# Running sums spread over the partitions by DMAs instead of matmuls, and three changes of order, in a two-part float32 network

## The chip, the cores and the metric

One core of a Trainium2 chip. The metric is the device time of one launch in microseconds, the median over several runs.

## The reference

The input is a sequence of 256 rows of 1024, with 16 learned rows ahead of it in the first part. Two attention layers (an indexer chooses up to 64 keys for each query; one key and value head serves eight query heads; a pooled branch and gates are merged in) are followed by a block of feed-forward, mixer, cross-attention and feed-forward parts. All is float32. The piece of the mixer that the change touches:

```python
x = (xh * dt[..., None]); la = dt * a           # 32 heads in 4 groups, 2 chunks of 128 positions
acs = jnp.cumsum(la, axis=-1)                   # the running sums, per head and chunk
seg = acs[..., :, None] - acs[..., None, :]
decay = jnp.exp(jnp.where(causal, seg, -jnp.inf))
y_diag = jnp.einsum('bcgls,bcgkls,bcsgkp->bclgkp', cb, decay, x)
y_off = jnp.einsum('bclgn,bcgkpn,bcgkl->bclgkp', cc, prev, jnp.exp(acs))
```

## The kernel before, in words

Channels lie on partitions, positions on columns. All weights stream once from HBM as 387 slots of 8 tiles of 128x128 (SyncE, L297). Each slot is split into two float32r parts: ScalarE copies the high part (`whi`, L310), GpSimd subtracts for the low part (`wlo`, L318), up to four slots ahead of TensorE. A `block` is one output tile: 8 (or more) weight tiles, each with three matmuls (high by high L358, high by low L359, low by high L360), or in the wide form two (L385, L388). A block takes one of four main PSUM banks, in rotation, and its `by` names the event that frees the bank. The other four banks (`side_`) serve everything else, also in rotation.

Each engine runs its own program, in order, written out by generators. Work beside the blocks (rotations, attention, the mixer's state part) is a list of generators `side`, and `tick(side)` lets each take one step between two blocks. So the place of a step in an engine's queue is set by the number of `yield`s, the same on all engines by hand.

The change touches these places.

- **The start of the first layer** (`layer_tensor`, l = 0): the blocks go keys, values, first index queries, then the rest. `rope_vector` (L711 scaling, L717 to L722 rotation) frees the keys' bank at its last instruction; `values_vector` (L768) frees the values' bank at once and, two yields on, scales the index weights (L773), for which it waits for ScalarE (L780).
- **Attention** (`attend_scalar`): for each pair of heads an exponential (L924) and, two steps later, the copies of the transposed probabilities (L930, L931) that the second product (L895) reads. One step of the program holds the exponentials of one pair and the copies of another.
- **The mixer's running sums.** `steps_vector` computes `acs`, 32 heads by 256 positions (L1607). ScalarE and VectorE split it in two float32r parts (`acr`, L1637, L1612).
- **The mixer's groups** (`ssd_*`, four groups of eight heads). For each pair of heads (`hp`, one per tick) TensorE multiplies a one-hot column with `acr` and so puts the head's sums on all partitions of a side bank (L1773, two matmuls). ScalarE takes four Relu of differences from it (L1916), an exponential in the bank (L1921) and one of the Relus' results (L1922). VectorE multiplies both (L1843, L1848). Group g runs beside the blocks of group g + 1.
- **The blocks beside it** are six `cv` blocks in three pairs and four `z` blocks. For a pair of `cv` blocks VectorE computes a convolution of four taps (L1706 to L1717), ScalarE a tanh (L1728), VectorE the product (L1734), which frees the bank. In `mixer_scalar` the tanh of the pair before stands behind the tick.

Of the kernel before, what the change touches and what calls it, by code (L numbers as in the profile page):

```python
# [13 lines left out]
T = 272  # L14
# [132 lines left out]
class Scalar(Engine):  # L147
    def begin(self, real):
        self.real, self.activation = real, real.activation
        return self  # L150
# [79 lines left out]
def build(tens, sems, known, wts, small, par, con, mem, out):  # L230
# [531 lines left out]
    def values_vector(e, K):  # L762
# [6 lines left out]
        yield  # L769
        yield  # L770
# [146 lines left out]
    def attend_scalar(e, K, t):  # L917
# [3 lines left out]
        for s in range(8):  # L921
            for hh in (2 * s - 2, 2 * s - 1) if 1 <= s < 5 else ():
                e.wait_ge(*v_step.of("max", l, t, s - 1))
                e.activation(K.L[:, hh, 0:nk], K.L[:, hh, 0:nk], ACT.Exp, bias=K.nm[:, hh:hh + 1],  # L924
                             accum_out=K.sm[:, hh:hh + 1]).then_inc(*s_step.done("exp", l, t, hh))
            for hh in (2 * s - 6, 2 * s - 5) if 3 <= s < 7 else ():
# [5 lines left out]
                    *s_out.done("pt", l, t, hh))  # L932
            yield
# [525 lines left out]
    def ffn_scalar(e, K):  # L1459
# [38 lines left out]
    (zacc, xs0, xs1, bc0, bc1, zs0, zs1, xdt, btok, xw, prev, M, E8, cv0, cv1, cv2, mt0, mt1, mt2, tokm, dtde, acol) = arena(  # L1498
        (8, S), (4, S), (4, S), (2, S), (2, S), (4, S), (4, S), (2, 512), (128,), (512,), (512,), (8, 256),
        (8, 128), (S,), (S,), (S,), (S,), (S,), (S,), (5, 32), (32,), (1,))  # L1500
# [4 lines left out]
    acr, idr = tens["acr"][:, 0:S], tens["acr"][:, S:S + 32]  # L1505
# [54 lines left out]

    def steps_tensor(e):
# [10 lines left out]
    def steps_vector(e):  # L1572
# [38 lines left out]
        e.wait_ge(*s_high.of("acr"))  # L1611
        e.tensor_tensor(acr[32:64, :], acs, acr[0:32, :].bitcast(F), ALU.subtract).then_inc(*v_low.done("acr"))  # L1612
# [6 lines left out]
    def steps_scalar(e):  # L1619
# [11 lines left out]
        e.wait_ge(*v_step.of("acs", 1))  # L1631
        e.activation(dq[:, 0:128], acs[:, 0:128], ACT.Exp, scale=-1.0, bias=acs[:, 127:128]).then_inc(*s_step.done("dden"))
# [108 lines left out]
    def ssd_tensor(e, g):  # L1741
# [25 lines left out]
        for hp in range(4):  # L1767
            o = side_.take(e, "seg", g, hp)
            side_.give(("seg", g, hp), (v_step, ("EC", g, hp)))
            e.wait_ge(*v_low.of("acr"))  # L1770
            for i in range(2):
                hd = 8 * g + 2 * hp + i
                m = e.matmul(o[:, S * i:S * i + S], idr[:, hd:hd + 1].broadcast_to([64, 128]), acr, start=True, stop=True)  # L1773
            m.then_inc(*piece.done("seg", g, hp))
            yield
# [39 lines left out]
    def ssd_vector(e, g):  # L1815
# [24 lines left out]
        for hp in range(5):  # L1840
            if hp:
                e.wait_ge(*s_step.of("E", g, hp - 1))
                e.tensor_tensor(E8[:, 2 * hp - 2:2 * hp, :], later(side_.at("seg", g, hp - 1)), ctb, ALU.mult).then_inc(  # L1843
                    *v_step.done("EC", g, hp - 1))
# [49 lines left out]
    def later(o):  # L1894

        return o.rearrange("p (a s) -> p a s", a=2)[:, :, 128:256]

    def ssd_scalar(e, g):
# [11 lines left out]
        for hp in range(4):  # L1910
            o = side_.at("seg", g, hp)
            e.wait_ge(*piece.of("seg", g, hp))
            for i in range(2):
                for c in range(2):
                    hd = 8 * g + 2 * hp + i
# [146 lines left out]
    def mixer_scalar(e):  # L2062
# [466 lines left out]
```

## Time and profile before

| | |
|---|---|
| median of 3 runs | 1271.03 us (1267.33 to 1271.29) |
| the profiled execution | 1270.99 us, span 1269.2 us |
| TensorE matmul, weight load | busy 98%, 90% |
| VectorE, ScalarE, GpSimd | busy 48%, 56%, 77% |
| DMA | 208.58 MB, 164 GB/s |
| mean granted TensorE clock | 0.995 |

A busy TensorE is one with a matmul in flight; how densely they follow is seen only from their starts in the timeline. The busy time of the other engines is summed over stages: in the mixer's groups VectorE and ScalarE are busier than these means.

### The profile page before, as it was taken

The page shows a single profiled execution, that of the slowest core. Times are in us where ns is not written, and L with a number is a line of the kernel's source. Part 1 is how long each engine was busy: PE and PEld are TensorE (multiplying, and loading weights), DVE is VectorE, ACT ScalarE, POOL GpSimd, SP SyncE. Part 2 cuts the span into 40 slices and gives each one's busy share as a digit, 9 for nine tenths or more (in the row PEclk, how much of TensorE's full clock was granted, in tenths as well). Part 3 has the DMA queues.
Part 4 walks back from the last instruction along what each step waited for, and adds up shares of the span by engine and source line. Part 5 has one row for each costly group of instructions (what it writes and reads, how often), then busy time and mean ns, then how long its engine had stood idle before and what let it go on. Part 6 is the DMA issues. An engine that isn't in the chain of part 4 may idle for free.

```text
span 1269.2 us, 22533 instructions
## 1 busy us (share of the span) xinstructions
PE 1241.6 (98%) x8950; PEld 1141.5 (90%) x8950; DVE 609.7 (48%) x1489; ACT 716.0 (56%) x1347; POOL 978.8 (77%) x774
## 2 busy tenths in 40 slices
PE   6999999999999999999999999999999999999997
PEld 5899899998889888889999999999999888888886
DVE  4476754456656444422755666632135234444312
ACT  5455656465556666545554676674447446666532
POOL 4567658767568999989799766769889767899894
PEclk9999999999999999999999999999999999999999
DMA  6334335444345555555465444445556434555552
GB/s 233 124 126 158 131 129 183 152 148 150 117 135 192 188 183 190 190 181 186 150 200 200 150 134 136 151 147 180 179 176 223 157 125 157 184 190 191 173 194 81
DMA packets 57784, 208.58 MB, mean 164 GB/s; under 512 B 6352, under 2 KB 7632, under 8 KB 57552
## 3 DMA queue, kind: packets, MB, share of 16 engines
q1 hardware_dynamic: 57680, 207.15, 49.2%
q8 instruction: 71, 1.16, 0.4%
q14 instruction: 33, 0.27, 0.1%
HBM read 206.07 MB, written 1.05 MB: 163 GB/s over the span
## 4 chain that ended last, share of the span: by engine, by line
PE 91%; DVE 4%; ACT 2%; issue 1%; DMA 1%; SPq 0%; POOL 0%; DVEq 0%
PE bank L385 22%; PE bank L358 17%; PE bank L360 16%; PE bank L359 16%; PE bank L388 11%; PE bank L895 1%; PE bank L699 1%; PE bank L1789 1%; ACT whi L310 1%; PE bank L905 1%; DMA raw<-w_dram 1%; PE bank L2166 1%; PE bank L2138 1%; PE bank L837 1%; PE bank L2188 1%
## 5 line engine op out<-in xcount | busy, mean ns | idle before, releaser
L318 POOL TENSOR_TENSOR wlo<-raw,whi 128x512 fp32r<-128x512 f32 x770 | 978.6, 1300 | 275.1 <-ACT whi L310 273.3
L310 ACT ACTIVATE whi<-raw 128x1024 fp32r<-128x1024 f32 x387 | 404.3, 1053 | 33.5 <-DMA raw<-w_dram 11.8
L358 PE MATMUL bank<-xx,whi 128*128 128x256 f32 (+1 forms) x1296 | 378.9, 292 | 12.0 <-DVE xx L448 9.4
L360 PE MATMUL bank<-xx,wlo 128*128 128x256 f32 (+1 forms) x1296 | 368.8, 285 | 0.0
L359 PE MATMUL bank<-xx,whi 128*128 128x256 f32 (+1 forms) x1296 | 368.6, 284 | 0.0
L358 PEld LDWEIGHTS bank<-xx,whi 128*128 128x128 f32 x1296 | 246.4, 190 | 21.3 <-issue 11.7
L360 PEld LDWEIGHTS bank<-xx,wlo 128*128 128x128 f32 x1296 | 246.8, 190 | 0.0
L359 PEld LDWEIGHTS bank<-xx,whi 128*128 128x128 f32 x1296 | 246.3, 190 | 0.5
L385 PE MATMUL bank<-xx,whi 128*128 128x512 f32 x704 | 178.9, 396 | 0.0
L358 PE MATMUL bank<-yy,whi 128*128 128x256 f32 (+1 forms) x524 | 151.2, 289 | 0.0
L360 PE MATMUL bank<-yy,wlo 128*128 128x256 f32 (+1 forms) x524 | 148.9, 284 | 0.0
L359 PE MATMUL bank<-yy,whi 128*128 128x256 f32 (+1 forms) x524 | 148.7, 284 | 0.0
L385 PEld LDWEIGHTS bank<-xx,whi 128*128 128x128 f32 x704 | 126.2, 188 | 23.8
L385 PE MATMUL bank<-yy,whi 128*128 128x512 f32 x476 | 121.6, 394 | 0.0
L388 PEld LDWEIGHTS bank<-xx,wlo 128*128 128x128 f32 x704 | 95.2, 188 | 8.0
L358 PEld LDWEIGHTS bank<-yy,whi 128*128 128x128 f32 x524 | 99.8, 190 | 2.6 <-issue 2.5
L385 PEld LDWEIGHTS bank<-yy,whi 128*128 128x128 f32 x476 | 85.4, 189 | 16.3 <-DVE yy L2212 0.5
L359 PEld LDWEIGHTS bank<-yy,whi 128*128 128x128 f32 x524 | 99.8, 190 | 0.1
L360 PEld LDWEIGHTS bank<-yy,wlo 128*128 128x128 f32 x524 | 99.8, 190 | 0.0
L388 PE MATMUL bank<-xx,wlo 128*128 128x256 f32 x704 | 97.4, 280 | 0.0
L1433 DVE TENSOR_TENSOR bank<-bank,ar 128x256 f32<-128x256 f32 x88 | 38.0, 432 | 123.2 <-ACT ar L1464 123.0
L1464 ACT ACTIVATE ar<-bank 128x256 f32<-128x256 f32 x88 | 33.8, 384 | 66.8 <-PE bank L388 66.8
(276 smaller groups left out, 1412.8 us busy)
## 6 DMA issues: line engine op xcount, KB each, us to landing
raw<-w_dram SPq DMA_DIRECT2D x387, 512.0 KB, 3.3
h<-x_dram SPq DMA_DIRECT2D x2, 544.0 KB, 6.2
ar<-mem_dram SPq DMA_DIRECT2D x1, 1024.0 KB, 5.6
out_dram<-h SPq DMA_DIRECT2D x4, 256.0 KB, 2.2
cst<-con_dram SPq DMA_DIRECT2D x1, 721.0 KB, 9.6
cst<-con_dram SPq DMA_DIRECT2D x1, 134.0 KB, 3.4
prm<-par_dram SPq DMA_DIRECT2D x1, 131.0 KB, 3.2
```

The source lines that it names most:

```text
L310: e.activation(whi[:, i % NSPL, :], raw[:, i % NRAW, :], ACT.Copy).then_inc(*whi_done.done(i))
L318: return e.tensor_tensor(wlo[:, q, c0:c1], raw[:, i % NRAW, c0:c1], whi[:, q, c0:c1].bitcast(F), ALU.subtract)
L358: e.matmul(o, wh, both[:, 0, :], start=(i == 0), stop=False)
L359: e.matmul(o, wh, both[:, 1, :], start=False, stop=False)
L360: m = e.matmul(o, wl, both[:, 0, :], start=False, stop=(i == len(feed) - 1))
L385: e.matmul(sums, tiles[-1][3], both, start=(i == 0), stop=(i == end))
L388: m = e.matmul(o[:, 0:n], wl, both[:, 0, :], start=False, stop=(i == end), skip_group_check=True)
L699: e.matmul(o, cst[:, C_PERM:C_PERM + 128], x, start=True, stop=True).then_inc(*piece.done("perm", l, kind, b))
L837: e.matmul(o, K.qiT[p0:p0 + 64, hh // 2, c0:c0 + 128], K.kiT[p0:p0 + 64, 0:nk], start=True, stop=True).then_inc(*piece.done("ix", l, t, hh))
L895: m = e.matmul(ob[half:half + 64, 128 * (hh // 2):128 * (hh // 2) + 128], K.V[0:kn, vi, 0:64], K.PT.at(l, t, hh)[0:kn, i, :], start=(i == ...
L1433: e.tensor_tensor(a, a, K.low.at(kind, K.key, j), ALU.add).then_inc(*v_step.done("sum", kind, K.key, j))
L1464: e.activation(b, K.sums(kind, j)[1], ACT.Copy).then_inc(*s_out.done("low", kind, K.key, j))
```

## The change

Running sums: ScalarE writes `acs` to a DRAM buffer once, and for each pair of heads a DMA from ScalarE's queue reads two rows back onto all 128 partitions, into one of three new buffers, three pairs ahead (`load_run`). The matmuls (L1773) and the split of the sums go. The Relus and the exponential read that buffer; the exponential writes to `E8`, and VectorE multiplies `E8` in place.

Tanh first: `mixer_scalar` puts the tanh of the pair before ahead of the tick. Attention: the copies stand ahead of the exponentials in each step. First layer (l = 0): the values' block comes ahead of the keys', and in both layers the scaling of the index weights comes four yields later. The second layer's blocks keep their order.

```diff
@@ values_vector
-        yield
-        yield
+        for _ in range(6):
+            yield
@@ attend_scalar: the loop of the exponentials is moved behind the loop of the copies
@@ layer_tensor
+    def keys_tensor(e, K):
+        l = K.l
+        block(e, ("kk", l, 0), "w_in", l, [(512, 64, 0), (2688, 64, 64)], K.x_all, T, by=[(v_step, ("rope", l, "kk", 0))])
...
-        block(e, ("kk", l, 0), "w_in", l, [(512, 64, 0), (2688, 64, 64)], K.x_all, T, by=[(v_step, ("rope", l, "kk", 0))])
         if l:
+            keys_tensor(e, K)
             norm_sums(e, N)
         block(e, ("v", l), "w_in", l, [(576, 64, 0), (2752, 8, 64)], K.x_all, T)
         if l == 0:
+            keys_tensor(e, K)
             norm_sums(e, N)
@@ mixer
+    def load_run(e, n):
+        if n < 16:
+            if n >= 3:
+                e.wait_ge(*s_step.of("fall", *divmod(n - 3, 4)))
+                e.wait_ge(*s_step.of("E", *divmod(n - 3, 4)))
+            e.dma_start(runs[n % 3], sums[2 * n:2 * n + 2, :].partition_broadcast(128)).then_inc(sems[f"run{n % 3}"], 16)
@@ steps_scalar
         e.wait_ge(*v_step.of("acs", 1))
+        e.dma_start(sums, acs).then_inc(sems["l_a"], 16)
...
-        e.activation(acr[0:32, :], acs, ACT.Copy).then_inc(*s_high.done("acr"))
-        for i in (0, 1):
-            e.activation(idr[32 * i:32 * i + 32, :], ident[0:32, 0:32], ACT.Copy).then_inc(*s_high.done("idr", i))
+        e.wait_ge(sems["l_a"], 16)
+        for n in range(3):
+            load_run(e, n)
@@ ssd_tensor
         for hp in range(4):
-            o = side_.take(e, "seg", g, hp)
...
-                m = e.matmul(o[:, S * i:S * i + S], idr[:, hd:hd + 1].broadcast_to([64, 128]), acr, start=True, stop=True)
             yield
@@ ssd_vector
-                e.tensor_tensor(E8[:, 2 * hp - 2:2 * hp, :], later(side_.at("seg", g, hp - 1)), ctb, ALU.mult).then_inc(
+                m = E8[:, 2 * hp - 2:2 * hp, :]
+                e.tensor_tensor(m, m, ctb, ALU.mult).then_inc(*v_step.done("EC", g, hp - 1))
@@ ssd_scalar
-            e.wait_ge(*piece.of("seg", g, hp))
+            n = 4 * g + hp
+            o = runs[n % 3]
+            e.wait_ge(sems[f"run{n % 3}"], 16 * (n // 3 + 1))
...
-            e.activation(rise, rise, ACT.Exp).then_inc(*s_step.done("E", g, hp))
+            e.activation(E8[:, 2 * hp:2 * hp + 2, :], o[:, :, 128:256], ACT.Exp).then_inc(*s_step.done("E", g, hp))
             e.activation(M[:, 2 * hp:2 * hp + 2, :], M[:, 2 * hp:2 * hp + 2, :], ACT.Exp, scale=-1.0).then_inc(
                 *s_step.done("M", g, hp))
+            load_run(e, n + 3)
@@ mixer_scalar
                     split_for(e, "cv", cb)
-                    tick(side)
                     silu_scalar(e, due)
                     due = ()
+                    tick(side)
```

ScalarE in the first group's head pairs, before (a `whi` row is a split of weights; L1728 is the tanh of a pair of `cv` blocks; `piece` is an event of TensorE, `v_out` one of VectorE, `w0` the landing of a weight slot):

```order
L1916 ACTIVATE ar<-bank,ar 128x128 [waits piece]
L1916 ACTIVATE ar<-bank,ar 128x128 x3
L1921 ACTIVATE bank<-bank 128x2x128 [waits s_step]
L1922 ACTIVATE ar<-ar 128x512
L310 ACTIVATE whi<-raw 128x1024 [waits w0]
L1916 ACTIVATE ar<-bank,ar 128x128 [waits piece]
L1916 ACTIVATE ar<-bank,ar 128x128 x3
L1921 ACTIVATE bank<-bank 128x2x128 [waits s_step]
L1922 ACTIVATE ar<-ar 128x512
L1728 ACTIVATE ar<-bank 128x256 [waits v_out] x2
```

The same place after the change (L1920, L1923, L1925 are the Relus and the two exponentials, L1743 the tanh, `run0` the landing of a load of the sums):

```order
L1920 ACTIVATE ar<-ar 128x128 [waits run0]
L1920 ACTIVATE ar<-ar 128x128 x3
L1923 ACTIVATE ar<-ar 128x256
L1925 ACTIVATE ar<-ar 128x512 [waits s_step]
L1573 DMA ar<-sums_dram 128x512 [waits s_step]
L310 ACTIVATE whi<-raw 128x1024 [waits w0]
L1743 ACTIVATE ar<-bank 128x256 [waits v_out] x2
L1920 ACTIVATE ar<-ar 128x128 [waits run1]
L1920 ACTIVATE ar<-ar 128x128 x3
L1923 ACTIVATE ar<-ar 128x256
```

The tanh pair moved from behind the second head pair to ahead of it, the wait for TensorE became one for a landing, and a DMA issue follows each pair.

VectorE in the first layer's start, before (L711 scales a block, L717 to L722 are a rotation, L773 the scaling of the index weights):

```order
L768 TENSOR_TENSOR ar<-bank,rows 72x272 [waits product]
L711 TENSOR_TENSOR bank<-bank,rows 128x272 [waits product]
L773 TENSOR_SCALAR ar<-ar 128x2x8 [waits s_out]
L711 TENSOR_TENSOR bank<-bank,rows 128x272 [waits product]
L717 TENSOR_TENSOR ar<-bank,cst 128x272 [waits piece]
L719 SCALAR_TENSOR_TENSOR bank<-bank,prm,cst 128x272
L722 TENSOR_TENSOR ar<-ar,bank 128x272 [waits v_step]
```

After:

```order
L768 TENSOR_TENSOR ar<-bank,rows 72x272
L711 TENSOR_TENSOR bank<-bank,rows 128x272 [waits product] x2
L717 TENSOR_TENSOR ar<-bank,cst 128x272 [waits piece]
L719 SCALAR_TENSOR_TENSOR bank<-bank,prm,cst 128x272
L722 TENSOR_TENSOR ar<-ar,bank 128x272 [waits v_step]
```

L773 left its place ahead of the keys' rotation. On TensorE the third index-query block, at the same time, before (`wlo_done` is the low part of the weights, `v_step` here the end of the keys' rotation):

```order
L758 MATMUL bank<-cst,ar 128x72 x2
L699 MATMUL bank<-ar,cst 128x272 [waits s_step]
L358 MATMUL bank<-xx,whi 128x272 [waits wlo_done,v_step]
L359 MATMUL bank<-xx,whi 128x272
L360 MATMUL bank<-xx,wlo 128x272
```

After:

```order
L758 MATMUL bank<-cst,ar 128x72 x2
L699 MATMUL bank<-ar,cst 128x272 [waits s_step]
L358 MATMUL bank<-xx,whi 128x272 [waits wlo_done]
L359 MATMUL bank<-xx,whi 128x272
L360 MATMUL bank<-xx,wlo 128x272
```

The block no longer waits for VectorE.

## Rows read from the trace of the kernel before

**Rows 1.** The page, part 4: the chain that ended last, by engine.

```profile
PE 91%; DVE 4%; ACT 2%; issue 1%; DMA 1%; SPq 0%; POOL 0%; DVEq 0%
```

**Rows 2.** Waits of TensorE: engine, line, releaser; us in total, times, longest.

```profile
PE bank L895 <- ACT ar L931: 1.1, 2, 0.7
```

**Rows 3.** Timeline of TensorE, blocks without side work: start us, us, instruction.

```profile
693.22 0.28 PE L358 MATMUL bank<-xx,whi 128*128 128x256 f32 x1
...
696.06 0.28 PE L358 MATMUL bank<-xx,whi 128*128 128x256 f32 x1
```

**Rows 4.** The same timeline beside the first group's head pairs.

```profile
709.79 0.50 PE L1773 MATMUL bank<-acr 64*128 64x256 f32 x2
710.22 0.39 PE L358 MATMUL bank<-xx,whi 128*128 128x256 f32 x1
...
717.11 0.39 PE L358 MATMUL bank<-xx,whi 128*128 128x256 f32 x1
...
720.55 0.39 PE L358 MATMUL bank<-xx,whi 128*128 128x256 f32 x1
...
723.51 0.38 PE L358 MATMUL bank<-xx,whi 128*128 128x256 f32 x1
```

**Rows 5.** Timeline of ScalarE in the same stretch.

```profile
712.36 1.05 ACT L310 ACTIVATE whi<-raw 128x1024 fp32r<-128x1024 f32 x1
713.79 1.14 ACT L1916 ACTIVATE ar<-bank,ar 128x128 f32<-128x128 f32 x4 [0.38 <-PE bank L1773]
714.97 0.37 ACT L1921 ACTIVATE bank<-bank 128x256 f32<-128x256 f32 x1
...
715.77 0.65 ACT L1728 ACTIVATE ar<-bank 128x256 f32<-128x256 f32 x2
```

**Rows 6.** Single lines: count, ns min/median/max; the last, of 700:850: busy, mean ns.

```profile
L1929 ACT ACTIVATE ar<-ar x8: 406/408/409, 731.4 to 845.2; 128x256 f32<-128x256 f32 x8
...
L1843 DVE TENSOR_TENSOR ar<-bank,ar x16: 411/418/425, 712.0 to 835.8; 128x256 f32<-128x256 f32 x16
...
L1891 DVE TENSOR_TENSOR yy<-ar,yy x16: 408/419/1520, 750.3 to 866.2; 128x256 fp32r<-128x256 f32 x16
...
L1891 DVE TENSOR_TENSOR yy<-ar,yy 128x256 fp32r<-128x256 f32 x12 | 6.4, 574 | 1.7 <-ACT yy L1946 1.7
```

**Rows 7.** Timeline of VectorE in the stretch of rows 4.

```profile
717.77 0.22 DVE L1706 TENSOR_SCALAR ar<-bank,prm 128x3 f32<-128x3 f32 x1
...
720.49 0.87 DVE L1717 SCALAR_TENSOR_TENSOR bank<-bank,prm,ar 128x256 f32<-128x256 f32 x2
...
721.61 0.68 DVE L1848 TENSOR_TENSOR ar<-ar,bank 128x512 f32<-128x512 f32 x1
723.04 0.75 DVE L1734 SCALAR_TENSOR_TENSOR ar<-ar,bank 128x256 f32<-128x256 f32 x2 [0.75 <-ACT ar L1728]
```

**Rows 8.** The line of the weights' DMAs: issue ns; us to landing.

```profile
L297 SPq DMA_DIRECT2D raw<-w_dram x387: 327/328/997, 0.7 to 1241.4; - x194
...
DMA to landing us min/median/max: 3.1/3.3/10.1
```

**Rows 9.** Timeline of TensorE and of VectorE at the first layer's start.

```profile
32.95 0.39 PE L358 MATMUL bank<-xx,whi 128*128 128x272 f32 x1 [2.12 <-DVE ar L722]
...
30.69 0.63 DVE L773 TENSOR_SCALAR ar<-ar 128x16 f32<-128x16 f32 x1 [3.34 <-ACT ar L780]
```

**Rows 10.** Stretches: us, PE, PEld, DVE, ACT, POOL busy (instructions), granted clock, DMA share, GB/s.

```profile
34.00:38.00 4.00, 4.00 (x21) 3.96 (x20) 0.32 (x2) 0.00 (x0) 1.65 (x2) 0.57 0.34 103
...
314.00:318.00 4.00, 4.00 (x23) 4.00 (x22) 0.14 (x1) 0.00 (x0) 2.40 (x2) 0.57 0.23 76
```

**Rows 11.** Timeline of TensorE and of ScalarE in the second layer's attention.

```profile
350.57 0.94 PE L905 MATMUL bank<-cst,ar 128*16 128x128 f32 x6
...
354.19 0.52 ACT L924 ACTIVATE ar<-ar 128x272 f32<-128x272 f32 x1 [0.23 <-DVE ar L947]
...
355.22 0.25 ACT L930 ACTIVATE ar<-bank 16x128 f32<-16x128 f32 x1
```

More of the change, by code:

```diff
@@ L227, in tick, with build @@
             side.remove(g)
-def build(tens, sems, known, wts, small, par, con, mem, out):
+def build(tens, sems, known, wts, small, par, con, mem, out, sums):
     P, V, A, G, Y = Tensor("pe"), Vector("dve"), Scalar("act"), Pool("pool"), Sync("sp")
@@ L932, in attend_scalar @@
                     *s_out.done("pt", l, t, hh))
+            for hh in (2 * s - 2, 2 * s - 1) if 1 <= s < 5 else ():
+                e.wait_ge(*v_step.of("max", l, t, s - 1))
+                e.activation(K.L[:, hh, 0:nk], K.L[:, hh, 0:nk], ACT.Exp, bias=K.nm[:, hh:hh + 1],
+                             accum_out=K.sm[:, hh:hh + 1]).then_inc(*s_step.done("exp", l, t, hh))
             yield
@@ L1504, in build @@
     dtu, dtv, dtw = (M[0:32, i, :] for i in (0, 1, 2))
-    acr, idr = tens["acr"][:, 0:S], tens["acr"][:, S:S + 32]
+    runs = [sg[:, 2 * k:2 * k + 2, :] for k in range(3)]
     cwh, cbh, snh = (prm[:, PARAMS[n]:PARAMS[n] + w] for n, w in (("cw", 96), ("cb", 24), ("sn", 16)))
@@ L1767, in ssd_tensor @@
         for hp in range(4):
-            o = side_.take(e, "seg", g, hp)
[L1769 to L1772, printed above, removed]
-                m = e.matmul(o[:, S * i:S * i + S], idr[:, hd:hd + 1].broadcast_to([64, 128]), acr, start=True, stop=True)
-            m.then_inc(*piece.done("seg", g, hp))
             yield
@@ L1910, in ssd_scalar @@
         for hp in range(4):
[L1911 to L1912 removed]
+            n = 4 * g + hp
+            o = runs[n % 3]
+            e.wait_ge(sems[f"run{n % 3}"], 16 * (n // 3 + 1))
             for i in range(2):
                 for c in range(2):
[L1915 to L1917 removed]
+                    m = e.activation(M[:, 2 * hp + i, 128 * c:128 * c + 128], o[:, i, 128 * c:128 * c + 128],
+                                     ACT.Relu, scale=-1.0, bias=tokm[:, 2 + c, 2 * n + i:2 * n + i + 1])
             m.then_inc(*s_step.done("fall", g, hp))
[L1919 removed]
+            e.activation(E8[:, 2 * hp:2 * hp + 2, :], o[:, :, 128:256], ACT.Exp).then_inc(*s_step.done("E", g, hp))
             e.wait_ge(*s_step.of("fall", g, hp))
[L1921 removed]
             e.activation(M[:, 2 * hp:2 * hp + 2, :], M[:, 2 * hp:2 * hp + 2, :], ACT.Exp, scale=-1.0).then_inc(
                 *s_step.done("M", g, hp))
+            load_run(e, n + 3)
             yield
@@ L2414, with program @@
           "wlo_done"]
-LOADS = ["l_h", "l_h2", "l_c1", "l_c", "l_p", "l_m", "o"] + [f"w{i}" for i in range(NRAW)]
-def program(nc, wts_shape_decl, small, par, con, mem, out):
+LOADS = ["l_h", "l_h2", "l_c1", "l_c", "l_p", "l_m", "l_a", "run0", "run1", "run2", "o"] + [f"w{i}" for i in range(NRAW)]
+def program(nc, wts_shape_decl, small, par, con, mem, out, sums):
     with ExitStack() as ctx:
@@ L2428, in program @@
             "cst": sb("cst", [128, NCONST]), "prm": sb("prm", [128, NPARAM]), "ar": sb("ar", [128, ARENA]),
-            "acr": sb("acr", [64, S + 32], R), "sq": sb("sq", [128, 2, T]), "rows": sb("rows", [128, 2, T]),
+            "sq": sb("sq", [128, 2, T]), "rows": sb("rows", [128, 2, T]),
             "banks": [ctx.enter_context(nc.psum_tensor(f"bank{i}", [128, 512], F)) for i in range(8)],
         }
-        plan, counted, engines = build(tens, sems, None, None, small, par, con, mem, out)
+        plan, counted, engines = build(tens, sems, None, None, small, par, con, mem, out, sums)
         for name in ("tensor", "vector", "scalar", "pool", "sync"):
@@ L2435, in program @@
         nslots = -(-len(plan) // TILES)
-        _, _, engines = build(tens, sems, counted(), wts_shape_decl(nslots), small, par, con, mem, out)
+        _, _, engines = build(tens, sems, counted(), wts_shape_decl(nslots), small, par, con, mem, out, sums)
         block = ctx.enter_context(nc.Block())
@@ L2472 @@
     mem, out = dram("mem_dram", [128, 8, S]), dram("out_dram", [128, 8, S], "ExternalOutput")
-    plan, nslots = program(nc, lambda n: dram("w_dram", [n, 128, SLOT]), small, par, con, mem, out)
+    sums = dram("sums_dram", [32, S], "Internal")
+    plan, nslots = program(nc, lambda n: dram("w_dram", [n, 128, SLOT]), small, par, con, mem, out, sums)
     mats = {
```

18 lines of the change are left out of this document (3 added, 15 removed).

## The prediction

> **What bounds the kernel now.** I read the chain of waits first: 91% of the span is TensorE, spread over the lines of the weight matmuls [rows 1]. So the question for every part of the change is whether it takes columns or a stall out of TensorE's queue, and whether another engine then holds it up at once. Next the waits of TensorE: they are few, and of those that the change can touch one stands in its own row, the attention's second product waiting for copies of ScalarE, 1.1 us in two places [rows 2]. Third the timeline of the mixer, where the change removes instructions.
>
> **The broadcasts by matmul.** Without side work a block of 24 matmuls takes 2.84 us (693.22 to 696.06) [rows 3]. With two broadcast matmuls behind it, it takes 3.44 us (717.11 to 720.55) [rows 4]; that is 0.60 us for one pair, the switch between their kind of operand and the blocks' included. There are 16 pairs. In each of the four groups the first pair stands behind the state matmul, whose own switch stays, so there I count only the pair itself, 709.79 to 710.22, 0.43 us [rows 4]. Gross: 12 x 0.60 + 4 x 0.43 = 8.9 us of TensorE's queue.
>
> **How much of it is kept.** Banks limit it. The four main banks go round, so the block that begins at 723.51 needs the bank of the block that began at 710.22 [rows 4]. VectorE frees that bank with the first of the two L1734 at 723.04, half of 0.75 us, near 723.4 [rows 7]: there is nothing to spare today. Four pairs earlier, TensorE would be there at 723.51 - 0.43 - 3 x 0.60 = 721.3. When is the bank free then? ScalarE: split of weights from 712.36, 1.05 us; then in the new order both tanh at once, 0.65 us, so to about 714.1. Now the second head pair; it took from 713.79 to 715.77, 1.98 us [rows 5]. Its four Relu and its exponential now read SBUF; the nearest pair of rows is 0.37 us for an exponential from PSUM [rows 5] and 0.41 for a square from SBUF [rows 6], so I add 0.04 for each of five and call it 2.2: to 716.3. VectorE multiplies the decays (the second of the two 0.68 us, L1848 [rows 7]), to 717.0, and its convolution of the next pair of blocks takes what it took from 717.77 to 721.36, 3.6 us [rows 7]: to 720.6. Behind it come again the two multiplications, which ended 0.93 us after the convolution (722.29 against 721.36), and the first L1734, 0.4 us [rows 7]; with 0.16 for a port wait (next part) the bank is free at about 722.1 to 722.2. TensorE waits some 0.9, say 1.0 us, for it in each of groups 0 to 2. The last group runs beside the merge gates' blocks, whose banks ScalarE alone frees: no stall. Kept: 8.9 - 3.0 = **5.9 us**. The ends are 8.9 (no stall) and 2.3 (as if those three groups kept today's cadence: 8.9 less 3 x 2.2).
>
> **The multiplication in SBUF (L1843).** It read PSUM and SBUF, 0.42 us and never over 0.43. Now both inputs lie in SBUF, where GpSimd works most of the time. The nearest row is L1891, the same operation and size with two SBUF inputs: median 0.42, longest 1.52 us, and a mean of 0.57 [rows 6]. I take the mean, 0.16 more, and hold 1.1 more for the range. The Trainium skill, in "SBUF — State Buffer", section "SBUF: two separate sides", says that such a VectorE instruction and a GpSimd one exclude each other for a whole instruction. By that rule this change puts 16 exclusions into the tightest chain of the mixer. Row L1891 agrees, with its 1.52 against 0.42; taken at its full length each time, the rule makes the time that of rival 3.
>
> **The transfers.** Three loads of 256 KB follow the write of the sums, and 13 more come one for each head pair, each three head pairs ahead, thus at least 3 x 2.84 = 8.5 us before use. A weight tile of 512 KB lands in 3.3 us, the slowest transfer of that line in 10.1 [rows 8]. I take them as hidden behind those three blocks; if one took 10.1 us, ScalarE would wait 1.6 us for it, up to 21 us for 13. The same 2 KB go to 128 partitions, which no row shows. An issue takes 0.33 us on SyncE [rows 8]; on ScalarE it stands behind the exponential of 512 columns that is still running, so I take 0, the other end being 16 x 0.33 = 5 us on an engine that is off the chain except in the three stalls above (there 3 x 0.33 us each at worst). In exchange two copies and two fills on ScalarE go and one subtraction on VectorE; they bounded nothing, 0 us.
>
> **The first layer's start.** TensorE idles 2.12 us before the block at 32.95 until L722, the end of the keys' rotation [rows 9]: that block, the third of the index queries, takes the bank of the first block, which was the keys'. With the values' block first, that bank is free when the values are scaled, long before. The keys' bank is then wanted one block later, 3 us on, and VectorE reaches the rotation earlier too, as it no longer stands 3.34 us idle before L773 [rows 9], which moves behind. Gain **2.1 us**, with no new waiter. Behind this idle time the granted clock falls to 0.57 over 34 to 38 us [rows 10], between its levels of 2.4 and 1.2 GHz. 4 us at 0.57 are 1.7 us lost. Without the idle time ahead I expect no fall: **1.7 us**, likely but not sure. In the second layer, the keys stay first; 0.
>
> **Copies before exponentials.** The transposes of the first heads ran at 350.57, ScalarE took the exponentials at 354.19 and the copies at 355.22 [rows 11], and TensorE waited for those. Turned round, the copies end about 1.0 us earlier. Both places of [rows 2] have this form: **1.1 us**. The later exponentials are read one block later; 0.
>
> **The sum.** 5.9 + 2.1 + 1.7 + 1.1 = 10.8 us. The profiled execution took 1270.99 us, beside its span of 1269.2, and the median is 1271.03, so one base serves both: 1271.0 - 10.8 = **1260.2 us**.
>
> **Rivals.**
> 1. The clock falls all the same, or at another place: the fall near 314 us [rows 10] stands behind another idle time, that the change does not touch: what lets a fall come is not in my hands. Then 1261.9. Chance 0.15.
> 2. The saved matmuls are only waited out: the three groups keep their cadence, since VectorE and ScalarE hand the banks over with nothing to spare. For it: the 723.4 against 723.51. Against: the tanh no longer stands behind a head pair, and the head pairs no longer wait for TensorE. Time: 1271.0 - (2.3 + 2.1 + 1.7 + 1.1) = 1263.8. Chance 0.12.
> 3. The port: every such multiplication loses 1.1 us. Two lie in each of the three critical chains, so the stall grows by about 2 us a group: 1260.2 + 6 = 1266.2. Against: the mean of L1891 is far from its longest. The rule of the page above would let GpSimd be held up too; no wait for it stands in this stage today. Chance 0.05.
> 4. Slower: the loads land late. ScalarE then stands at its wait in front of the Relu with the next tanh and the next split of weights behind it, so the banks stay taken and TensorE stops. It decides from 8.5 us of landing on; the gain of 10.8 us is used up when 13 loads each cost 0.83 us, thus at 9.3 us, and it is over 0.3% slower at about 9.6. At 10.1 us: 1260.2 + 21 = 1281. For it: a landing of 10.1 exists [rows 8]. Against: the median is 3.3 for twice the bytes. Chance 0.04. "DMA: Bandwidth & Descriptors" of the Trainium skill, section "Latency and other measured facts", gives HBM access as 0.2 us on average and 2 at high load; this would leave the loads hidden, and no row of this kernel shows such a broadcast.
> 5. The forecast itself keeps 0.64.
>
> **How the numbers follow.** 0.3% is 3.8 us, about what a measurement of this kernel can tell from no change. Rivals 1 and 2 and most of the forecast lie below 1267.2. Range: down to 1255.5, where the 3.0 us of stall and the second clock fall (1.7) are gone as well; up to 1266.0, where rivals 1 and 2 come together (1265.5) with a little of the port. Within 0.3% lie rival 3 together with 1 or 2 (1267.9 and more), a mild form of 4, and what I have not thought of: 0.06. Slower is rival 4, 0.04, and faster the rest, 0.90.
>
> **What would show it.** Right: no broadcast matmul, a block pitch near 2.84 us in the head pairs, and one TensorE wait of about 1 us in each of three groups, ended by L1734's successor; no wait at 31 us, and a granted clock of 1.00 there; no wait for the copies at 127 and 356 us. Run loads landing in 2 to 5 us. Wrong: ScalarE idle until a load of the sums; multiplications of 0.42 us that last over 1 us in most cases; a new stall of TensorE outside the cv blocks, or a total above 1267.

## The result, and the profile after

| | before | after |
|---|---|---|
| median of 5 runs, us | 1270.62 (1267.33 to 1271.29) | 1263.48 (1261.66 to 1264.37) |
| ratio to before, 95% interval | | 0.9948 [0.9931, 0.9964] |
| profiled execution: span / time, us | 1269.2 / 1270.99 | 1262.3 / 1264.1 |

The change makes the kernel 0.5% faster; 7.1 us by the medians, 6.9 us by the two spans. The forecast was 10.8 us, to 1260.2. The result lies inside the range of 1255.5 to 1266.0, but 3.3 us above the value itself. Two terms make that distance: stalls of TensorE that are longer than forecast, which can be read and in part undone, and a gain in granted clock that did not come.

The page of the changed kernel, part 4 (the chain that ended last, by engine), against [rows 1]: VectorE's share rose from 4% to 6%.

```profile
PE 90%; DVE 6%; ACT 2%; issue 1%; DMA 1%; SPq 0%; POOL 0%; DVEq 0%
```

Waits of TensorE after the change (engine, line, releaser; us in total, times, longest). The row of [rows 2], L895 waiting for the copies, and the wait for L722 of [rows 9] are gone. A wait of 5.5 us in three places is new.

```profile
PE bank L358 <- DVE ar L1749: 5.5, 3, 2.0
```

Timeline of TensorE in the first group, and the same stall in the next two groups. The blocks beside the head pairs now follow one another in 2.84 us (710.34 to 713.18), the pitch of a bare block in [rows 3], where [rows 4] had 3.44. The next block should then begin at 713.18 + 2.84 = 716.02; it begins at 717.61, **1.59 us late**. The same reckoning gives 2.18 us in groups 1 and 2, thus 5.95 us in all. (The idle time in the rows is a little less, since the previous matmul is counted busy to its end.)

```profile
710.34 0.28 PE L358 MATMUL bank<-xx,whi 128*128 128x256 f32 x1
...
713.18 0.28 PE L358 MATMUL bank<-xx,whi 128*128 128x256 f32 x1
...
717.61 0.38 PE L358 MATMUL bank<-xx,whi 128*128 128x256 f32 x1 [1.43 <-DVE ar L1749]
...
755.14 0.38 PE L358 MATMUL bank<-xx,whi 128*128 128x256 f32 x1 [2.02 <-DVE ar L1749]
...
794.25 0.38 PE L358 MATMUL bank<-xx,whi 128*128 128x256 f32 x1 [2.02 <-DVE ar L1749]
```

Timeline of VectorE ahead of the first of these stalls, the stretch that answers to [rows 7]. The first of the two L1749 (the multiplication with the tanh, L1734 before) frees the bank. Ahead of it stand the convolution, then L1852 and L1856 (L1843 and L1848 before). This L1852 lasts 1.26 us in place of 0.42, and the one ahead of the convolution 0.86.

```profile
710.49 0.86 DVE L1852 TENSOR_TENSOR ar<-ar 128x256 f32<-128x256 f32 x1 [0.99 <-ACT ar L1923]
...
714.59 0.87 DVE L1732 SCALAR_TENSOR_TENSOR bank<-bank,prm,ar 128x256 f32<-128x256 f32 x2
715.37 1.26 DVE L1852 TENSOR_TENSOR ar<-ar 128x256 f32<-128x256 f32 x1
716.55 0.67 DVE L1856 TENSOR_TENSOR ar<-ar,bank 128x512 f32<-128x512 f32 x1
717.15 0.74 DVE L1749 SCALAR_TENSOR_TENSOR ar<-ar,bank 128x256 f32<-128x256 f32 x2
717.81 0.41 DVE L1852 TENSOR_TENSOR ar<-ar 128x256 f32<-128x256 f32 x1
```

The groups of VectorE by line (count; busy us, mean ns; idle before): the mean of L1852 is 698 ns. L1899 is the line that was L1891 in [rows 6].

```profile
L1899 DVE TENSOR_TENSOR yy<-ar,yy 128x256 fp32r<-128x256 f32 x16 | 13.7, 893 | 1.6 <-ACT yy L1950 1.6
L1852 DVE TENSOR_TENSOR ar<-ar 128x256 f32<-128x256 f32 x16 | 11.2, 698 | 5.4 <-ACT ar L1923 5.4
```

What makes an L1852 long shows when GpSimd's low parts of the weights (L318) are laid beside it. First GpSimd, then VectorE, in group 1 of the changed kernel.

```profile
752.60 1.27 POOL L318 TENSOR_TENSOR wlo<-raw,whi 128x512 fp32r<-128x512 f32 x1 [0.45 <-ACT whi L310]
753.84 1.45 POOL L318 TENSOR_TENSOR wlo<-raw,whi 128x512 fp32r<-128x512 f32 x1
```

```profile
752.83 1.32 DVE L1852 TENSOR_TENSOR ar<-ar 128x256 f32<-128x256 f32 x1
```

L1852 begins 0.23 us behind the start of a GpSimd instruction that ends at 753.87, and ends at 754.15, 0.28 us later. This is no accident of one place. I laid all 32 executions of L1852 and L1899 beside GpSimd's. Half of them, 16, begin while an L318 runs and has over 0.15 us left: each of these ends 0.279 to 0.286 us behind the end of that L318. The other 16 take 0.409 to 0.426 us. So the duration of such an instruction is not a spread around a mean; it is set by how much of GpSimd's instruction is left when it begins. Laid out in the same way, the nine traces of this document hold 111 such instructions that begin inside an L318, and 109 of them end 0.277 to 0.287 us behind it. The other two are in `tick_first`, one each in groups 1 and 2: they are recorded as beginning 0.07 us behind the L318, take their 0.41 us, and it is the L318 that takes 1.64 us. So at such a distance the record of the starts does not tell which of the two will be held up; another L1852 of that kernel, 0.07 us behind its L318, took 1.52 us.

```profile
756.63 1.64 POOL L318 TENSOR_TENSOR wlo<-raw,whi 128x512 fp32r<-128x512 f32 x1 [1.60 <-ACT whi L310]
```

```profile
756.71 0.41 DVE L1852 TENSOR_TENSOR ar<-ar 128x256 f32<-128x256 f32 x1
```

The transfers, by the line of their issue (issue ns min/median/max; us to landing): they were as hidden as taken, with no wait for them anywhere.

```profile
L1573 ACTq DMA_DIRECT2D ar<-sums_dram x16: 326/327/454, 644.9 to 820.6; - x16
...
DMA to landing us min/median/max: 3.4/4.0/5.1
```

The granted clock in the profiled execution of the changed kernel (stretches as in [rows 10]) is 1.00 at 34 us and at 310 to 318 us, where the one of before had its two falls, but 0.62 at 26 to 30 us and 0.57 at 756 to 760 us. That makes two falls ahead of the last blocks before and two after, at other places; a share of 1.00 is the level of 2.4 GHz, and within a fall the clock is at 1.2 GHz.

```profile
22.00:26.00 4.00, 2.28 (x15) 1.91 (x14) 2.22 (x9) 1.46 (x3) 2.67 (x4) 0.95 0.74 236
26.00:30.00 4.00, 4.00 (x22) 4.00 (x22) 1.14 (x3) 2.17 (x5) 2.39 (x2) 0.62 0.43 154
...
34.00:38.00 4.00, 4.00 (x33) 3.92 (x32) 2.08 (x6) 1.34 (x2) 2.77 (x3) 1.00 0.23 58
310.00:318.00 8.00, 7.72 (x61) 6.28 (x62) 3.42 (x10) 4.16 (x15) 2.54 (x2) 1.00 0.41 133
752.00:756.00 4.00, 1.98 (x17) 1.77 (x16) 4.00 (x9) 3.96 (x10) 2.84 (x3) 1.00 0.67 236
756.00:760.00 4.00, 4.00 (x25) 3.87 (x25) 3.86 (x11) 1.75 (x4) 3.61 (x3) 0.57 0.67 200
```

### The profile page after: what moved, and what is told of

Read it like the earlier page. It is cut to its first block, busy times and chain, and to the rows that moved or that the text cites. A ratio compares the mean times of both kernels' runs of the same rounds, so it can differ in the third digit from the quotient of the medians.

```text
span 1262.3 us, 22496 instructions
## 1 busy us (share of the span) xinstructions
PE 1232.8 (98%) x8918; PEld 1137.6 (90%) x8918; DVE 613.1 (49%) x1488; ACT 717.0 (57%) x1344; POOL 979.5 (78%) x774
## 4 chain that ended last, share of the span: by engine, by line
PE 90%; DVE 6%; ACT 2%; issue 1%; DMA 1%; SPq 0%; POOL 0%; DVEq 0%
PE bank L385 22%; PE bank L358 16%; PE bank L360 15%; PE bank L359 15%; PE bank L388 11%; PE bank L895 1%; PE bank L699 1%; PE bank L905 1%; ACT whi L310 1%; PE bank L1797 1%; PE bank L912 1%; DVE ar L1727 1%; DMA raw<-w_dram 1%; PE bank L2170 1%; PE bank L2142 1%
## 5 line engine op out<-in xcount | busy, mean ns | idle before, releaser
L318 POOL TENSOR_TENSOR wlo<-raw,whi 128x512 fp32r<-128x512 f32 x770 | 979.3, 1300 | 267.0 <-ACT whi L310 265.1
L358 PE MATMUL bank<-xx,whi 128*128 128x256 f32 (+1 forms) x1296 | 379.2, 293 | 15.4 <-DVE xx L448 9.5
L358 PEld LDWEIGHTS bank<-xx,whi 128*128 128x128 f32 x1296 | 247.0, 191 | 23.4 <-issue 12.6
L358 PE MATMUL bank<-yy,whi 128*128 128x256 f32 (+1 forms) x524 | 151.2, 289 | 0.0
L358 PEld LDWEIGHTS bank<-yy,whi 128*128 128x128 f32 x524 | 99.8, 190 | 2.6 <-issue 2.5
```

What stands on the lines that cost most here:

```text
L318: return e.tensor_tensor(wlo[:, q, c0:c1], raw[:, i % NRAW, c0:c1], whi[:, q, c0:c1].bitcast(F), ALU.subtract)
L358: e.matmul(o, wh, both[:, 0, :], start=(i == 0), stop=False)
```

## The experiments

Seven kernels, in two sets. The first four (`mixer_only` to `e_psum`) ran beside 17 executions of the kernel before with a median of 1269.06 us, the last three beside 23 with 1270.56 us; in the result's own runs it was 1270.62. So a comparison between a kernel of these sets and the changed kernel is safer by the ratios to before than by the medians; where both are given they differ by up to 1.1 us. Every kernel computes the whole reference. Theory A is: the changed kernel's distance from the forecast is the new stall, the stall is set by L1749's place in VectorE's queue, and L1852, with both inputs in SBUF, makes the stall long by waiting for GpSimd.

### The mixer's part alone, and the rest alone

`mixer_only`, from the changed kernel:

```diff
@@ values_vector
-        for _ in range(6):
-            yield
+        yield
+        yield
@@ attend_scalar: the loop of the exponentials goes back ahead of the loop of the copies
@@ layer_tensor
+        keys_tensor(e, K)
...
-            keys_tensor(e, K)
```

> The change with the first layer's start and the attention's order undone; only the mixer's part (sums by DMA, tanh first) is left. Theory A (the traces of before and after add up part by part): three TensorE stalls of 1.6, 2.2 and 2.2 us ahead of the first z block, and the mixer gives 3.9 us of its 8.9, less or more 1.5 for a clock fall. The waits at 31 us (2.1) and for the copies (0.7 and 0.35) are back. Time about 1270.6 - 3.9 = 1266.7, 1.5 less or more by where the clock falls. Rival B (the mixer's part is a loss and the other two edits carry the gain): not below 1270.

Measured: 1267.05 us (11 runs), ratio to before 0.9984 [0.9974, 0.9994], span 1265.0. Waits of TensorE:

```profile
PE bank L358 <- DVE ar L1748: 5.5, 3, 2.0
...
PE bank L358 <- DVE ar L722: 1.7, 1, 1.7
...
PE bank L895 <- ACT ar L931: 1.1, 2, 0.7
```

`start_attn`, from the kernel before, is the complement: the values' block first, L773 later, copies first, and nothing of the mixer.

```diff
@@ values_vector
-        yield
-        yield
+        for _ in range(6):
+            yield
@@ attend_scalar: the loop of the exponentials is moved behind the loop of the copies
@@ layer_tensor
-        block(e, ("kk", l, 0), "w_in", ...)
+        def keys():
+            block(e, ("kk", l, 0), "w_in", ...)
         if l:
+            keys()
...
         if l == 0:
+            keys()
```

> The kernel before with the two other edits alone: values' block ahead of the keys' and L773 later, copies ahead of exponentials. Theory A: the idle time of 2.1 us at 31 us and the two of 0.7 and 0.35 for the copies are gone, 3.4 us with the 0.2 around them, 1267.2. The clock falls once for 3.4 us soon after the idle time at 23 us instead of at 34 us, so that term gives 0, not 1.7; whether the fall at 314 us stays is open (1.5 us). Rival B (removing the idle time removes a fall as well, as I had forecast): granted clock 1.00 from 24 to 40 us and about 1265.5.

Measured: 1265.69 us (5 runs), ratio 0.9968 [0.9956, 0.9981], span 1264.1. Both waits are gone, and the second fall of the clock with them; the first one only moved ahead, to 26 us:

```profile
26.00:30.00 4.00, 4.00 (x22) 4.00 (x21) 1.14 (x3) 2.08 (x5) 2.41 (x3) 0.57 0.39 137
310.00:318.00 8.00, 7.72 (x61) 6.29 (x61) 3.31 (x10) 4.15 (x14) 2.54 (x2) 1.00 0.41 132
```

What follows: the two halves are 0.16% and 0.32%, together 0.48%, against 0.52% for the whole change; they add up. The mixer's half, with 5.9 of the forecast's 10.8 us, is the smaller one on the chip. The three stalls belong to it alone and do not depend on the rest. By the ratio the mixer's half gains 2.0 us (0.8 to 3.3) where 3.9 was expected; the time of 1267.05 came near the expected 1266.7 only because the kernel before was 1.6 us faster in this set. Laid beside before, the profiled execution does gain 4.0 us between 700 and 866 us, and it loses elsewhere: TensorE's clock stays low for 6.8 us from 311.7 us, against 3.4 us before. `start_attn` went as theory A expected, with the fall at 314 us gone besides, which had been left open.

### The tanh behind the side work again

`tick_first` keeps the loads but takes back the order of ScalarE:

```diff
@@ mixer_scalar
                     split_for(e, "cv", cb)
+                    tick(side)
                     silu_scalar(e, due)
                     due = ()
-                    tick(side)
```

> The change with the tanh of the pair before behind the head pair again. Theory A (the tanh's place counts, since the bank is freed by the product behind it): in the first group the tanh of the first pair comes at about 710.5 instead of 708.3 and that of the second about as late as 717.9 instead of 715.1, so the bank of the 12th block is free about 1 to 2 us later: stalls of 2.5 to 4 us in each of three groups, and 3 to 5 us more than the change in all. Rival B (VectorE alone sets the release, since the tanh is done by the time its two multiplications are): stalls as in the change, within 0.5 us.

Measured: 1266.13 us (6 runs), ratio 0.9975 [0.9964, 0.9987]. Six stalls in place of three:

```profile
PE bank L358 <- DVE ar L1749: 7.7, 6, 1.9
```

and in group 1 VectorE waits for the tanh, with a long L1852 in the same round:

```profile
748.23 0.75 DVE L1749 SCALAR_TENSOR_TENSOR ar<-ar,bank 128x256 f32<-128x256 f32 x2 [2.27 <-ACT ar L1743]
748.90 0.76 DVE L1899 TENSOR_TENSOR yy<-ar,yy 128x256 fp32r<-128x256 f32 x2
749.57 1.52 DVE L1852 TENSOR_TENSOR ar<-ar 128x256 f32<-128x256 f32 x1
```

What follows: the due tanh first is worth about 2.7 us by the medians (1266.13 against 1263.48) and 3.4 by the ratios. Theory A's direction is right and its size at the lower end of what it said (3 to 5 us), but groups 1 and 2 each have two stalls, and group 0 stalls for less than the 2.5 us expected. Without the early tanh the removed matmuls bring 0.25% together with all the rest.

### One input of L1852 back in PSUM

`e_psum`: the exponential of the decays is written to the PSUM bank of the state matmul, free by then, and L1852 reads it there. The loads, the matmuls and the order stay those of the changed kernel; ScalarE gets one wait more, for the previous L1852 (at a group's first pair, for its own copy of the state product out of that bank).

```diff
@@ ssd_tensor
-        side_.give(("st", g), (s_out, ("prev", g)))
+        side_.give(("st", g), (v_step, ("EC", g, 3)))
...
@@ ssd_vector
-                m = E8[:, 2 * hp - 2:2 * hp, :]
-                e.tensor_tensor(m, m, ctb, ALU.mult).then_inc(*v_step.done("EC", g, hp - 1))
+                rise = side_.at("st", g)[:, 0:256].rearrange("p (a s) -> p a s", a=2)
+                e.tensor_tensor(E8[:, 2 * hp - 2:2 * hp, :], rise, ctb, ALU.mult).then_inc(*v_step.done("EC", g, hp - 1))
...
@@ ssd_scalar
+        rise = side_.at("st", g)[:, 0:256].rearrange("p (a s) -> p a s", a=2)
...
-            e.activation(E8[:, 2 * hp:2 * hp + 2, :], o[:, :, 128:256], ACT.Exp).then_inc(*s_step.done("E", g, hp))
+            e.wait_ge(*(v_step.of("EC", g, hp - 1) if hp else s_out.of("prev", g)))
+            e.activation(rise, o[:, :, 128:256], ACT.Exp).then_inc(*s_step.done("E", g, hp))
```

> The change with the exponential written to the state product's PSUM bank instead of SBUF, so that L1852 (the multiplication) reads PSUM and SBUF as before; nothing else moved. Theory A (the port shared with GpSimd makes L1852 long, 0.86 and 1.26 us in the first group): every L1852 lasts 0.41 to 0.43 us, the stalls shrink by 0.8 us or so each, from 1.6, 2.2, 2.2 to about 0.7, 1.3, 1.3, the time by 2 to 3 us. Rival B (those instructions are long for another reason, as a late exponential): still over 0.8 us in some, and stalls as before.

Measured: **1258.42 us** (4 runs), ratio 0.9912 [0.9895, 0.9929], span 1256.3: the fastest of all. The line of L1852, the waits, and one L1852 that begins inside an L318 (GpSimd's row behind it) and still takes 0.41 us:

```profile
L1852 DVE TENSOR_TENSOR ar<-bank,ar 128x256 f32<-128x256 f32 x16 | 6.7, 416 | 6.7 <-ACT bank L1925 6.7
```

```profile
PE bank L358 <- DVE ar L1749: 2.5, 3, 1.1
```

```profile
750.78 0.41 DVE L1852 TENSOR_TENSOR ar<-bank,ar 128x256 f32<-128x256 f32 x1
```

```profile
750.49 1.28 POOL L318 TENSOR_TENSOR wlo<-raw,whi 128x512 fp32r<-128x512 f32 x1 [0.41 <-ACT whi L310]
```

What follows: the place of one operand decides how long L1852 takes. The stalls shrink from 1.59, 2.18 and 2.18 us to 0.49, 1.25 and 1.25, by 2.96 us together, at the upper end of the 2 to 3 expected. The median is 5.1 us lower (4.6 by the ratios), and the span shrank by 6.0. Most of the rest is the clock: there is no fall in the mixer or at the start in the profiled execution,

```profile
26.00:30.00 4.00, 4.00 (x28) 3.41 (x28) 1.59 (x4) 2.44 (x5) 2.41 (x3) 1.00 0.39 125
...
756.00:760.00 4.00, 4.00 (x44) 3.70 (x41) 3.93 (x11) 2.19 (x5) 4.00 (x4) 1.00 0.68 245
```

and the same matmuls of the two traces, laid beside each other, gain about 1.4 us at 25 to 29 us and 1.6 us at 756 to 760 us; the first 20 us went 1.5 us slower in this execution and the idle time there about 1 us better. That the fall at 756 us vanished with the shorter stall (1.25 in place of 2.18 us) is seen; that it vanished because of it is likely, not shown. The one at 26 us lies in a place that the edit does not touch; it is also missing in the traces of `tick_first`, `prod_first` and `prod_first_psum`, whose first layer is the same, so it is no gain of this edit. The last 0.5 us is the end of the kernel (see the sum below).

### VectorE's order: the due multiplications ahead of the side work

`prod_first` (from the changed kernel) and `prod_first_psum` (the same edit on top of `e_psum`):

```diff
@@ mixer_vector
                 for cb in pair:
-                    tick(side)
                     silu_vector(e, due)
                     due = ()
                     tick(side)
+                    tick(side)
```

> The changed kernel, but VectorE does the multiplications with the due tanh (two L1749) ahead of both pieces of side work and not between them. Theory A (in groups 0 to 2 the bank is late because L1749 stands in VectorE's queue behind one L1852 and one L1856): the first L1749 follows its tanh and the convolution at once, 1.9 us earlier in group 0 (1.26 + 0.67 us less), the stalls of 1.6, 2.2 and 2.2 us shrink to 0, 0.5 and 0.5 us at most, and with them the clock has less cause to fall near 756 us. Time 1258 to 1260, ratio to the kernel before 0.990 to 0.992. Theory B (the stalls are set by ScalarE's tanh or by the convolution): L1749 gains under 0.5 us and the time stays at 1262 to 1264. Theory C: L1852, now behind, holds up the next sums of the head pairs, so that the time comes back at a later wait for piece or L1732: stalls gone at L358, new ones at L904 or the like; 1261 to 1264.

> The same with the exponential of the decays going to a PSUM bank, so that L1852 has one input in PSUM. With L1852 off the way of L1749, theory A gives it little more than prod_first: no stall in groups 0 to 2 at all; 1256 to 1258, ratio 0.988 to 0.990. If the port mattered only through L1749's place in the queue (theory A), the two kernels lie within 2 us of each other; if it also delays the head pairs by itself (theory B), this one is 3 us or more faster than prod_first.

Measured: `prod_first` 1269.14 us (12 runs), ratio 0.9988 [0.998, 0.9997], 5.7 us slower than the changed kernel (5.1 by the ratios) where theory A expected 1258 to 1260. `prod_first_psum` 1260.29 us (5 runs), ratio 0.9917 [0.9905, 0.993], no faster than `e_psum` and above the 1256 to 1258 expected. My theory A in its narrow form, that only L1749's place counts, is wrong, and this is where it fell. The timeline of TensorE in `prod_first`: the stall of group 0 is gone as expected, but those of groups 1 and 2 have doubled.

```profile
755.99 0.58 PE L358 MATMUL bank<-xx,whi 128*128 128x256 f32 x1 [4.14 <-DVE ar L1749]
...
798.00 0.38 PE L358 MATMUL bank<-xx,whi 128*128 128x256 f32 x1 [4.14 <-DVE ar L1749]
```

VectorE ahead of the first of them:

```profile
744.41 0.75 DVE L1749 SCALAR_TENSOR_TENSOR ar<-ar,bank 128x256 f32<-128x256 f32 x2 [1.25 <-ACT ar L1743]
745.08 2.12 DVE L1899 TENSOR_TENSOR yy<-ar,yy 128x256 fp32r<-128x256 f32 x2
747.12 0.41 DVE L1852 TENSOR_TENSOR ar<-ar 128x256 f32<-128x256 f32 x1
...
748.05 1.85 DVE L1899 TENSOR_TENSOR yy<-ar,yy 128x256 fp32r<-128x256 f32 x2
749.83 1.52 DVE L1852 TENSOR_TENSOR ar<-ar 128x256 f32<-128x256 f32 x1
...
754.58 0.87 DVE L1732 SCALAR_TENSOR_TENSOR bank<-bank,prm,ar 128x256 f32<-128x256 f32 x2
755.51 0.81 DVE L1749 SCALAR_TENSOR_TENSOR ar<-ar,bank 128x256 f32<-128x256 f32 x2
```

Two L1899 take 2.12 us where the changed kernel had 0.74 (744.35), and L1852 1.52 where it had 0.41 (748.40): 1.38 + 1.11 = 2.5 us. That is not all. TensorE began this group 1.27 us earlier in `prod_first` (739.97 against 741.24), so the convolution (L1721 at 751.87 against 749.33) is 3.8 us late by the blocks beside it. The other 1.25 us is VectorE's idle time in the first row above: the multiplications now stand first in the queue and their tanh is not done, so VectorE stands idle with all its side work behind them. The changed kernel used that time for L1899, L1852 and L1856. Of the 32 executions of L1852 and L1899, 20 now begin inside an L318, and all 20 end 0.279 to 0.285 us behind its end. With L1852's input in PSUM the same order keeps the wait for the tanh,

```profile
743.75 0.75 DVE L1749 SCALAR_TENSOR_TENSOR ar<-ar,bank 128x256 f32<-128x256 f32 x2 [1.24 <-ACT ar L1743]
```

but loses far less: its two stalls are 2.08 us by the pitch of the blocks, against 4.30 in `prod_first` and 1.25 in `e_psum`. The two kernels of one order are 8.8 us apart (1269.14 and 1260.29), the two of the other 5.1 us (1263.48 and 1258.42). Part of the 8.8 and of the 5.7 us is the clock: in the profiled executions it fell behind both stalls of `prod_first` (low for 6.8 us from 754.2 and 3.4 us from 798.6), behind one only in the changed kernel, and by the pitch of the blocks that is 2.3 us more lost, beside the 2.65 us more of stall. Theory C named a delay that comes back at a later wait; it came back at L358 itself, in the next groups. Theory B of the second expectation holds: waiting for GpSimd delays the side work by itself, wherever that stands.

### The loads issued late

`late_loads` takes the cover off the transfers, which cost nothing in the change:

```diff
@@ steps_scalar
-        for n in range(3):
+        for n in range(1):
             load_run(e, n)
...
@@ ssd_scalar
-            load_run(e, n + 3)
+            load_run(e, n + 1)
```

> The changed kernel, but the load of a pair of running sums is issued one head pair ahead of its use and not three. It has then some 2.84 us less 1 us, against a landing of 4.0 us. If rival 4's mechanism and price hold (ScalarE stands in front of the Relu with the next tanh and split behind it), each load is late by 1 to 2 us, ScalarE shows waits for the load at L1920, and TensorE stops for part of it: 5 to 20 us slower than the changed kernel, 1268 to 1284. If ScalarE has slack that takes the wait in most groups, under 3 us slower.

Measured: 1276.9 us (10 runs, 1269.63 to 1281.73), ratio 1.0045 [1.0029, 1.0061], thus 13.4 us slower than the changed kernel (12.3 by the ratios), as expected (5 to 20); the profiled execution, at 1271.59, is one of the quick ones. ScalarE waits for a load in 12 of 16 head pairs, 17.5 us together, and TensorE stops 4.1 us in the first group:

```profile
715.90 1.28 ACT L1920 ACTIVATE ar<-ar 128x128 f32<-128x128 f32 x4 [3.15 <-DMA ar<-sums_dram]
...
718.86 0.63 ACT L1743 ACTIVATE ar<-bank 128x256 f32<-128x256 f32 x2
...
720.32 1.28 ACT L1920 ACTIVATE ar<-ar 128x128 f32<-128x128 f32 x4 [0.84 <-DMA ar<-sums_dram]
```

```profile
719.73 0.58 PE L358 MATMUL bank<-xx,whi 128*128 128x256 f32 x1 [4.11 <-DVE ar L1749]
```

What follows: rival 4's mechanism is real, but it needs the distance of three head pairs to be lost. Its price, one us for each us that ScalarE waits, is an upper end: here 17.5 us of waits go with a span 7.5 us longer than the changed kernel's. The ten executions spread over 12 us. The landings (3.1 to 4.9 us in the profile) now stand in the chain, but the granted clock differs too, from 0.993 in the quickest to 0.986 in the slowest, and how much of the spread is whose is not shown. A side effect fits the rule of the 0.28 us: VectorE here waits for ScalarE's exponential, and so none of its 16 L1852 begins inside an L318; none is over 0.43 us.

## Why the prediction was right and where it was off

**The bound and the sign**: right. TensorE's queue was the bound, most of what was taken out of it came through, and the waits named as gone are gone.

**The start** (2.1 us) and **the copies** (1.1 us): right. Laying the same matmuls of the two traces beside each other, the lead is 2.3 us behind the start; the copies' two waits (1.1 us in `mixer_only`) are gone. `start_attn` shows them free of the mixer.

**The broadcasts' gross** (8.9 us): the mechanism right, the size slightly low. The changed kernel's lead grows by 0.9, 0.3, 0.3 and 2.4 us in the four groups; with the stalls of 1.59, 2.18, 2.18 and 0 added, each group saves 2.4 to 2.5 us gross against 2.23 taken, 9.8 us in all.

**How much is kept** (5.9 us): here the size was off, by 2.0 us. The stalls are where it put them, in groups 0 to 2 and not in the last, released by L1734's successor, but they total 5.95 and not 3.0 us, and the mixer keeps 0.9 + 0.3 + 0.3 + 2.4 = 3.9 us. Two steps of the reckoning were wrong:

- *The port term.* I took the mean of L1891 and charged 0.16 us a multiplication. The L1852 that stands in front of L1749 takes 1.26 us in group 0 and 1.32 in groups 1 and 2, 0.84 to 0.90 us more every time, since each group meets GpSimd in nearly the same phase. In group 0 the one ahead of the convolution is long too (0.86). A mean was the wrong statistic. It was also low: I took it from the 12 executions up to 850 us (574 ns), of which most lie free of GpSimd. The rows of before could have told: an instruction's start against GpSimd's, and 0.28 us behind its end for each that overlaps. The 7 executions of L1891 in before that begin inside an L318 follow that to 5 ns. `e_psum` measures the term: 2.96 us over the three groups. Rival 3 had the mechanism with a price of 1.1 for both multiplications of each chain; what came true is one long one per chain and a second, shorter one in group 0, a half of rival 3. The Trainium skill, in "SBUF — State Buffer", section "SBUF: two separate sides", says that a VectorE instruction with two SBUF inputs and a GpSimd one that reads SBUF take a port pair that both engines share, for a whole instruction, and the later one waits. These runs agree with it, with 0.41 us against 1.26 to 1.52, and with the 1.64 us of GpSimd's in `tick_first`.
- *One group worked, three multiplied.* I worked group 0 only. Groups 1 and 2 also carry the previous group's end, the L1899, two of which take 1.85 us in group 1. The convolution there begins 8.09 us behind the start of the group's first block, in group 0 7.57 us; with the 0.06 us that L1852 is longer, that is the 0.59 us between the stalls of 2.18 and 1.59. No run took the L1899 away, so that they are the cause is read from the order and not tested. With L1852's port wait gone, `e_psum` leaves 0.49 + 1.25 + 1.25 = 2.99 us of stall, as much as the 3.0 of the forecast: group 0 had been put too high and the other two too low, and that the two cancel is luck.

**The clock** (1.7 us): in the profiled executions wrong by its whole size; rival 1 is what happened. In place of the fall behind the removed idle time there is one behind the idle time before it (26 us), that at 314 us went away, which the prediction had said the change does not touch, and a new one stands behind the new stall of 2.18 us at 755. Two before, two after, about 1.5 us each: nothing gained. But each trace is one execution. Of the seven traces with the new start, three have the fall at 26 us, three others one at 310 us, and `e_psum` has neither. The mean granted clock of the kernel before ranged from 0.998 (1267.1 to 1268.2 us) to 0.994 (1270.3 to 1272.1) over its 40 executions beside the experiments, and that of the changed kernel from 0.997 (1261.66) to 0.994 (1264.37), and 0.995 is the most frequent value of the one and the middle one of the other. So the clock moves one execution by 3 us, as much as the terms argued over here, and what the change does to it is known only as about nothing on the median.

**The transfers and issues** (0): right; 3.4 to 5.1 us to landing against at least 8.5 us of distance, and ScalarE's 0.33 us issues lie inside the exponential of 512 columns.

The sum as measured: 2.3 + 1.1 + 3.9 + 0 = 7.3 us. The lead stays at 7.4 us to the last weight matmul, and the spans differ by 6.9; the last 0.5 us goes at the very end. There the clock falls in both kernels, before behind the last four matmuls (the granted clock is 1.00 from 1262.1 to 1262.9 us), and in the changed kernel just ahead of them (0.50 from 1254.7 to 1256.0). Before, then after:

```profile
1262.18 0.71 PE L528 MATMUL bank<-cst 128*128 128x128 f32 x4 [0.55 <-DVE cst L510]
```

```profile
1254.79 1.22 PE L528 MATMUL bank<-cst 128*128 128x128 f32 x4 [0.55 <-DVE cst L510]
```

Against the forecast of 10.8 us, 2.0 are missing in the mixer, 1.7 in the clock and 0.5 at the end, and 0.2 came on top at the start. Rivals 1 and 3, one of them by half, came together, a case for which the prediction held no chance of its own; the range took it in by rivals 1 and 2.

## What to carry to other kernels

When the second input of a VectorE instruction moves from PSUM to SBUF while GpSimd works, do not price it by a mean: lay its start against GpSimd's instructions, for every place where it stands in a chain, and count (for 256 columns, as here) 0.28 us behind the end of the one that it falls into. Work through every repetition whose surroundings differ. And an order that looks better by dependencies can be worse by phase, and by a wait that now stands in front of other work: here the "free" reorder of VectorE cost 5.7 us. Moving one result to a PSUM bank gained 5.1 us, about 3 us of it read as shorter stalls and the rest mostly a better granted clock. Compare two traces by the distance to the matmuls beside an instruction, not by the time since each one's start.

## What the runs showed of the hardware

- A VectorE tensor-by-tensor instruction of 256 columns with two SBUF inputs that begins inside a GpSimd instruction of the L318 kind and has over 0.15 us of it left ends 0.28 us behind it (36 of 36 in the changed kernel and `prod_first`, 109 of 111 in all nine traces), 1.52 us in the worst case; alone it takes 0.41 us, and with one input in PSUM it takes 0.40 to 0.43 us whatever GpSimd does. It works the other way too: the L318 that begins before such an instruction has ended takes 1.45 us instead of 1.27, and 1.64 in the two places of `tick_first`.
- The granted clock's falls that were looked at here follow idle times of TensorE, but not each idle time has one: behind the same kind of stall of 2.2 us there was a fall at 756 us and none at 794 us, and over the same first layer seven traces have a fall at 26 us in three and none there in four. `mixer_only` had 0.61 over 310 to 318 us where the kernel before had 0.79. What decides between them stays open. A fall of 3.4 us costs about 1.5 us here (the same matmuls in two traces, at 34, 314 and 756 us), so a measured gain of 2 or 3 us can hold one of them.
- A load of 256 KB that repeats the same 2 KB over 128 partitions lands in 4.0 us (3.4 to 5.1), somewhat slower than a weight tile of twice the bytes (median 3.3 us, up to 10.1).
